# Clearing layer 0's semaphores inside three later stages, on GpSimd

## The chip, the core and the metric

The kernel runs on one core of a Trainium2 chip. The core has five engines, each with an instruction queue of its own: TensorE (matmuls, PE in the profile), VectorE (DVE), ScalarE (ACT), GpSimd (POOL) and SyncE (SP, which here only issues DMAs). They meet only through semaphores. The metric is the time of one execution on the device in microseconds, as the median of several runs.

## The reference

The trunk has two layers over 512 latent tokens and 256 context tokens of width 1024. Layer 0 mixes tokens by a gated convolution, layer 1 by a bidirectional gated recurrence (HGRN2). Each is followed by a retrieval of single-neuron experts (PEER). Cut to what matters:

```python
for i in range(DEPTH):                       # DEPTH = 2
    hx = modulate(rms_norm(x, norm1_g[i]), mx[0], mx[1])
    if kind == 0:
        yx = short_conv_mixer(hx, conv_w_in[j], conv_k[j], conv_w_out[j], rows)
    else:
        yc, yx = hgrn2_mixer(hc, hx, hgrn_w_in[j], lower_bounds[i], hgrn_norm_g[j], hgrn_w_out[j])
    x = x + mx[2] * yx
    x = x + mx[5] * peer_ffn(modulate(rms_norm(x, norm2_g[i]), mx[3], mx[4]),
                             peer_w_q[i], peer_keys[i], peer_u[i], peer_v[i])
    ...                                      # the context tokens in the same way in layer 0
return rms_norm(x, final_g)
```

`peer_ffn` projects each token to queries, ranks 128 + 128 keys for each of 8 heads, takes the 16 best pairs, and sums over those experts a gate times GELU(u . h) times v. The semaphores of the change compute nothing.

## The kernel before

The kernel is a row of stages, one after the other: `stage_front`, `stage_conv`, `stage_rank`, `stage_gates` and `stage_experts` for layer 0, then `stage_hgrn`, `stage_mix_out`, `stage_rank`, `stage_gates` and `stage_experts` for layer 1, then `stage_final`. Each stage is one `nc.Block()`: a list of instructions for each engine, which begin together and end with a barrier (each engine drains, then all are released together). The line of the `with nc.Block()` statement is the line under which the trace has these drains and releases: 1363 for `stage_experts`, 1610 for `stage_hgrn`, 108 for the block in `retire`.

Inside a stage the engines are ordered by semaphores which count up and are waited for with constants. A stage takes its semaphores with `t.sem(name)`, which also puts them on the list `t.own`. Weights flow in 512 KB tiles: SyncE loads a tile into one of four buffers (`w_raw`, line 131), ScalarE makes its high part (`w_hi`, line 136), VectorE or GpSimd the low part (`w_lo`, line 147, the helper `t.lo`), and TensorE multiplies three times (lines 168 to 170; 1426 to 1428 in the experts). The first two tiles of a stage are prepared at the end of the stage before.

The semaphores of layer 0's five stages are used again in layer 1, and must be zero for that. `retire()` (lines 106 to 115) is called once, between the layers: it opens a block of its own in which GpSimd clears each semaphore of `t.own` with one instruction (line 113), then empties the list and gives the semaphores back.

GpSimd's work in the three stages that the change touches is this. In `stage_gates` it waits for the expert indices of 128 tokens (`idx_done`) and then issues one gather for each expert row (line 1298), paced by VectorE. In `stage_experts` it zeroes the sums (line 1403), issues 256 gathers (line 1407) in layer 0, waits until the stage's weight tiles are done (`t.lo_done`), and makes the low parts of the next stage's first two tiles. In `stage_hgrn` it fills masks (lines 1619 to 1638) and then makes low parts of weight tiles, up to the first two of `stage_mix_out`; TensorE, ScalarE and VectorE run a loop of 3 passes over 2 heads each, and the last two heads after it. `stage_experts` has on TensorE, ScalarE, VectorE and SyncE a loop over groups of four tiles; VectorE's has 31 passes.

`stage_hgrn` begins with a norm: ScalarE takes a square root (line 434), VectorE a reciprocal (line 453), and then, slice by slice of 128 channels, VectorE scales (line 448), ScalarE makes the high part (line 438), VectorE the low part (line 462), and TensorE multiplies the slice.

Of the kernel before, what the change touches and what calls it, by code (L numbers as in the profile page):

```python
# [55 lines left out]
class Trunk:  # L56
# [46 lines left out]
        self.own.append(self.own_ctx.enter_context(self.nc.semaphore(name)))  # L103
        return self.own[-1]

    def retire(self):

        with self.nc.Block() as block:

            @block.gpsimd  # L110
            def _(pool):
                for s in self.own:
                    pool.sem_clear(s)
        self.own = []
        self.own_ctx.close()

    def settle(self, eng):

# [822 lines left out]
def stage_gates(t, layer, tokens, top, top_i, h_tok, idx, weight, g_dram, act_dram):  # L941
# [24 lines left out]
    with ExitStack() as ctx:  # L966
# [59 lines left out]
        with nc.Block() as block:  # L1026
# [178 lines left out]
            def _(act):  # L1205
# [54 lines left out]
                for i in range(SPLIT, W):  # L1260
                    t.hi(act, i, i, i, 0)
                h_copy(0)
                ends = [0] + [end for end, _, _ in order]
                wide_at = [{ends[n] + (ends[n + 1] - ends[n]) * x // 13: n for n in range(blocks)} for x in (2, 6)]
                exp_at = {ends[n] + (ends[n + 1] - ends[n]) * 8 // 13: n for n in range(blocks)}
# [23 lines left out]

            @block.gpsimd  # L1290
            def _(pool):
                rows = t.a[f"peer_u_rows{layer}"].rearrange("j i d -> (j i) d")
                for d in range(dots):
                    if d % P == 0:
                        pool.wait_ge(idx_done, d // P + 1)
                    if d >= UBUF:
                        pool.wait_ge(u_used, d - UBUF + 1)
                    pool.indirect_dma_start(  # L1298
                        out=ubuf[:, d % UBUF], out_offset=None, in_=rows,
                        in_offset=bass.IndirectOffsetOnAxis(ap=idx[:, d // P, d % P:d % P + 1], axis=0)).then_inc(  # L1300
                            u_in[d % UBUF], 16)
# [33 lines left out]
def stage_experts(t, layer, tokens, idx, weight, g_dram, act_dram, nxt=None):  # L1335
# [10 lines left out]
    with ExitStack() as ctx:  # L1346
# [16 lines left out]
        with nc.Block() as block:  # L1363
# [36 lines left out]
            @block.gpsimd  # L1400
            def _(pool):
                rows = t.a[f"peer_v{layer}"].rearrange("j i d -> (j i) d")
                pool.memset(acc[:], 0.0).then_inc(sum_zero, 1)
                for d in range(S * n):
                    if d >= NB:
                        pool.wait_ge(v_used, S + d - NB + 1)
                    pool.indirect_dma_start(  # L1407
                        out=vbuf[:, d % NB], out_offset=None, in_=rows,
                        in_offset=bass.IndirectOffsetOnAxis(ap=idx[:, d % S, d // S:d // S + 1], axis=0)).then_inc(
                            v_in[d % NB], 16)  # L1410
                if nxt is not None:
                    pool.wait_ge(t.lo_done, n + (t.tiles + RAW))
                    for x in range(SPLIT):
                        t.lo(pool, n + x, x, x)
# [135 lines left out]
def stage_hgrn(t, y, nxt, sums):  # L1550
# [21 lines left out]
    with ExitStack() as ctx:  # L1572
# [25 lines left out]
        def turns(eng, turn):  # L1598


            with eng.Fori(0, HEADS // 2 - 1) as q:
                for u in range(2):
                    turn(q, u, 1)
            turn(HEADS // 2 - 1, 0, 2)
            turn(HEADS // 2 - 1, 1, 0)
# [4 lines left out]
        with nc.Block() as block:  # L1610

            @block.sync
            def _(sp):
                for i in range(SPLIT, n + SPLIT):
                    t.load(sp, t.a["hgrn_w_in"][i] if i < n else nxt(i - n), i, i % N_RAW, N_RAW, None)

            @block.gpsimd
            def _(pool):
                pool.memset(reset[:], 1.0).then_inc(S["reset_done"], 1)
                for d in range(2):  # L1620
                    pool.memset(same[d][:], 1.0).then_inc(S["mask_done"], 1)
                    pool.memset(probs[d][:], 0.0).then_inc(S["reset_done"], 1)
                pool.wait_ge(S["reset_done"], 3)
                pool.memset(av(reset)[:, :, 0:1], 0.0).then_inc(S["reset_done"], 1)

                m = 2
                for d in range(2):
                    sv = same[d][:].rearrange("p (c l) -> p c l", l=CHUNK)
                    sign = 1 if d == 0 else -1

                    pool.wait_ge(S["mask_done"], m)
                    pool.affine_select(out=sv, in_=sv, compare_op=ALU.is_ge, fill=0.0, base=0,
                                       pattern=[[sign * CHUNK, P // CHUNK], [sign, CHUNK]],
                                       channel_multiplier=-sign).then_inc(S["mask_done"], 1)
                    m += 1

                    pool.wait_ge(S["mask_done"], m)
                    pool.affine_select(out=sv, in_=sv, compare_op=ALU.is_ge, fill=0.0,
                                       base=0 if d == 0 else CHUNK - 1,
                                       pattern=[[-sign * CHUNK, P // CHUNK], [0, CHUNK]],  # L1640
                                       channel_multiplier=sign).then_inc(S["mask_done"], 1)
                    m += 1

                def lo(q, j):
                    t.lo(pool, q * BODY + j, j % N_RAW, j % SPLIT)

                def turn(q, u, more):

                    if more:
                        for i in range(PER):  # L1650
                            lo(q, PER * (u + 1) + SPLIT + i)
                for j in range(SPLIT, PER + SPLIT):
                    lo(0, j)
                turns(pool, turn)

            @block.tensor
            def _(pe):
# [297 lines left out]
def hybrid_trunk(nc, a):  # L1955

    with ExitStack() as ctx:
        t = Trunk(nc, ctx, a)
        dense = [T - S * P for T, S in zip((TOK, SEQ), SPARSE)]
        g_dram = [nc.dram_tensor(f"gates{i}", [GROUPS, P, T // STAGE_T, QUAD * STAGE_T], F32, kind="Internal").ap()  # L1960
                  for i, T in enumerate(dense)]
        act_dram = [nc.dram_tensor(f"acts{i}", [NKEYS, P, T], F32, kind="Internal").ap() for i, T in enumerate(dense)]
        tile = lambda name: lambda x: a[name][x]
        for layer, tokens in enumerate((TOK, SEQ)):
            with ExitStack() as mix:
                t.context_h(mix, f"m{layer}")
                if layer == 0:
                    stage_front(t, tile("conv_w_in"))
                    y_hi = mix.enter_context(nc.sbuf_tensor("y_hi", [P, KC, TOK], F32R))
                    y_lo = mix.enter_context(nc.sbuf_tensor("y_lo", [P, KC, TOK], F32R))  # L1970
                    sums = stage_conv(t, y_hi, y_lo, tile("peer_w_q0"))
                else:
                    y = mix.enter_context(nc.sbuf_tensor("y_heads", [P, KC, SEQ], F32))
                    stage_hgrn(t, y, tile("hgrn_w_out"), sums)
                    sums = stage_mix_out(t, layer, "hgrn_w_out", tokens, t.moving(SEQ), tile("peer_w_q1"), SPLIT, y)
            with ExitStack() as pick:
                S = SPARSE[layer]
                sb = lambda n, s, d=F32: pick.enter_context(nc.sbuf_tensor(f"{n}{layer}", s, d))
                idx, weight = sb("expert_idx", [P, S, P], U32), sb("expert_weight", [P, S, P])
                with ExitStack() as lists:  # L1980
                    sb = lambda n, s, d=F32: lists.enter_context(nc.sbuf_tensor(f"{n}{layer}", s, d))
                    h_tok = sb("h_tok", [P, S, D])
                    top, top_i = sb("top", [P, tokens // P, LISTS, TOPK]), sb("top_i", [P, tokens // P, LISTS, TOPK], U32)
                    with ExitStack() as h:
                        if tokens == TOK:
                            t.context_h(h, f"p{layer}")
                        stage_rank(t, layer, tokens, top, top_i, h_tok, tile(f"peer_u{layer}"), sums)
                    stage_gates(t, layer, tokens, top, top_i, h_tok, idx, weight, g_dram[layer], act_dram[layer])
                sums = stage_experts(t, layer, tokens, idx, weight, g_dram[layer], act_dram[layer],
                                     tile("hgrn_w_in") if layer == 0 else None)  # L1990
            if layer == 0:
                t.retire()
        stage_final(t, sums)


# [58 lines left out]
```

## Time and profile before

| what | us |
|---|---|
| median of 3 runs | 4148.39 |
| lowest and highest run | 4147.36, 4149.64 |
| span of the profiled execution | 4139.5 |
| TensorE matmuls busy in it | 3881.7 |

The span goes from the first to the last instruction of the profiled execution; what a run takes beyond it lies before and after the program's instructions. Times in the rows are microseconds from the span's start unless marked ns. In a wait, "A <- B" says that A stood idle until B; an engine's name with a q (SPq, POOLq) is its instruction queue: waits, drains, clears and the issuing of DMAs, which aren't counted as busy.

### The profile page before, as it was taken

To read this page: it belongs to the slowest core of one execution; us is meant where nothing else is said; L and a number is where in the kernel's file an instruction comes from. 1 tells how busy PE (TensorE), PEld (TensorE's weight loads), DVE (VectorE), ACT (ScalarE), POOL (GpSimd) and SP (SyncE) were. 2 spreads that over 40 slices of the span, in tenths; PEclk is the share of its full clock that TensorE was granted. 3 is DMA by queue.
4 is the path that set the end of the run, shared out by engine and by line. 5 is a ranking of instruction groups with operands and counts; after the bars stand their busy time and mean duration, and the time that the engine had idled before them with its cause. 6 is when DMAs were issued, how large, how long until landed. Compare 5 with 4: busy or idle time off the path is not lost. (4 is left out here: it accounts for less than half of the span.)

```text
span 4139.5 us, 63328 instructions
## 1 busy us (share of the span) xinstructions
PE 3881.7 (94%) x20946; PEld 3333.0 (81%) x20946; DVE 3194.6 (77%) x5918; ACT 1963.3 (47%) x3786; POOL 1169.6 (28%) x905
## 2 busy tenths in 40 slices
PE   8998988999999989999997999778899999899998
PEld 2787877788888868888886777657899999899997
DVE  2698789999997768888886555658998877677777
ACT  2212234777777722222223555433488887333333
POOL 0232212343443334444442222123122222122221
PEclk9999999999999999999999999979999999999999
DMA  7443116899999999999991111022589898899996
GB/s 295 163 162 113 46 54 216 305 326 334 331 341 339 334 358 372 375 373 377 373 373 60 55 46 46 31 77 66 183 299 308 308 309 312 306 333 332 333 332 219
DMA packets 411884, 1026.09 MB, mean 248 GB/s; under 512 B 33968, under 2 KB 182448, under 8 KB 405680
## 3 DMA queue, kind: packets, MB, share of 16 engines
q1 hardware_dynamic: 296496, 604.22, 41.5%
q0 software_dynamic: 110592, 402.70, 26.8%
q10 hardware_dynamic: 4608, 16.78, 1.1%
q8 instruction: 104, 1.70, 0.2%
q14 instruction: 84, 0.69, 0.0%
HBM read 904.03 MB, written 119.54 MB: 247 GB/s over the span
## 5 line engine op out<-in xcount | busy, mean ns | idle before, releaser
L136 ACT ACTIVATE w_hi<-w_raw 128x1024 fp32r<-128x1024 f32 x536 | 568.3, 1060 | 1174.1 <-PE psum L1428 881.9
L168 PE MATMUL psum<-h_hi,w_hi 128*128 128x512 f32 (+1 forms) x2208 | 853.0, 386 | 89.6 <-PEq L809 32.8
L170 PE MATMUL psum<-h_hi,w_lo 128*128 128x512 f32 (+1 forms) x2208 | 832.5, 377 | 0.0
L169 PE MATMUL psum<-h_lo,w_hi 128*128 128x512 f32 (+1 forms) x2208 | 832.3, 377 | 0.0
L147 DVE TENSOR_TENSOR w_lo<-w_raw,w_hi 128x1024 fp32r<-128x1024 f32 x424 | 519.4, 1225 | 387.2 <-ACT w_hi L136 366.7
L1426 PE MATMUL psum<-a_hie,w_hi 128*128 128x512 f32 (+1 forms) x2048 | 756.6, 369 | 31.0 <-DVE a_loe L1499 31.0
L1428 PE MATMUL psum<-a_hie,w_lo 128*128 128x512 f32 (+1 forms) x2048 | 756.7, 369 | 0.0
L1427 PE MATMUL psum<-a_loe,w_hi 128*128 128x512 f32 (+1 forms) x2048 | 754.1, 368 | 0.0
L1298 POOL DMA_INDIRECT u_rowsg<-in_peer_u_rows,expert_idx x384 | 446.1, 1162 | 1050.9 <-DVE u_rowsg L1053 919.4
L1407 POOL DMA_INDIRECT v_rowse<-in_peer_v,expert_idx x384 | 421.1, 1097 | 830.1 <-DVE row_sume L1508 816.9
L1228 ACT ACTIVATE ojg<-eq_jg,gate_Tg 128x128 fp32r<-128x128 bf16 x1792 | 550.2, 388 | 109.9 <-DVE eq_jg L1076 109.4
L147 POOL TENSOR_TENSOR w_lo<-w_raw,w_hi 128x1024 fp32r<-128x1024 f32 x116 | 295.3, 2546 | 973.4 <-ACT w_hi L136 973.4
L168 PEld LDWEIGHTS psum<-h_hi,w_hi 128*128 128x128 f32 x2208 | 419.4, 190 | 142.5 <-issue 45.8
L1508 DVE SCALAR_TENSOR_TENSOR row_sume<-v_rowse,expert_weight,row_sume 128x1024 f32<-128x1024 f32 x384 | 491.0, 1279 | 0.3 <-DMA v_rowse<-in_peer_v,expert_idx 0.3
L1053 DVE SCALAR_TENSOR_TENSOR u_rowsg<-u_rowsg,psum 128x1024 f32<-128x1024 f32 x384 | 462.7, 1214 | 11.1 <-DMA u_rowsg<-in_peer_u_rows,expert_idx 7.6
L170 PEld LDWEIGHTS psum<-h_hi,w_lo 128*128 128x128 f32 x2208 | 418.6, 190 | 63.7
L1426 PEld LDWEIGHTS psum<-a_hie,w_hi 128*128 128x128 f32 x2048 | 385.5, 188 | 94.0 <-DVE a_loe L1499 32.2
L169 PEld LDWEIGHTS psum<-h_lo,w_hi 128*128 128x128 f32 x2208 | 420.0, 190 | 35.1
L1427 PEld LDWEIGHTS psum<-a_loe,w_hi 128*128 128x128 f32 x2048 | 385.8, 188 | 52.3
L1428 PEld LDWEIGHTS psum<-a_hie,w_lo 128*128 128x128 f32 x2048 | 385.5, 188 | 44.4
L1192 PEld LDWEIGHTS psum<-ojg,eq_ig 128*128 128x128 f32 x1792 | 230.8, 191 | 41.3 <-ACT ojg L1228 32.8
L168 PE MATMUL psum<-h_hi,w_hig 128*128 128x512 f32 (+1 forms) x672 | 253.5, 377 | 1.0 <-DVE w_log L147 0.9
(263 smaller groups left out, 5474.5 us busy)
## 6 DMA issues: line engine op xcount, KB each, us to landing
w_raw<-in_peer_u SPq DMA_DIRECT2D x256, 512.0 KB, 6.0
w_raw<-in_peer_v SPq DMA_DIRECT2D x256, 512.0 KB, 5.4
gates<-stageg SPq DMA_DIRECT2D x28, 2048.0 KB, 15.9
acts<-act_gg SPq DMA_DIRECT2D x128, 256.0 KB, 5.1
gte<-gates SPq DMA_DIRECT2D x32, 1024.0 KB, 8.3
act_fe<-acts SPq DMA_DIRECT2D x128, 256.0 KB, 6.0
ada_w<-in_ada_w SPq DMA_DIRECT2D x12, 2048.0 KB, 8.7
ada_rows<-in_ada_w SPq DMA_DIRECT2D x48, 512.0 KB, 3.8
```

The source lines that it names most:

```text
L136: act.activation(self.weights(s)[0], self.raw[:, slot, :], ACT.Copy).then_inc(self.hi_done, 1)
L147: pool.tensor_tensor(lo, self.raw[:, slot, :], hi.bitcast(F32), ALU.subtract).then_inc(self.lo_done, 1)
L168: pe.matmul(out, wh, hi[:, k], start=(k == 0), stop=False)
L169: pe.matmul(out, wh, lo[:, k], start=False, stop=False)
L170: last = pe.matmul(out, wl, hi[:, k], start=False, stop=(k == KC - 1))
L1053: dve.scalar_tensor_tensor(out=row, in0=row, scalar=1.0, in1=h_row, op0=ALU.mult, op1=ALU.mult, accum_out=pre_act[:, s, r:r + 1]).then_inc ...
L1228: last = act.activation(oj[:, g % OJ, x, j], eq_j[:, g % EQ, j], ACT.Copy, scale=gate_T[:, b % 2, x, r + j:r + j + 1])
L1298: pool.indirect_dma_start(out=ubuf[:, d % UBUF], out_offset=None, in_=rows, in_offset=bass.IndirectOffsetOnAxis(ap=idx[:, d // P, d % P:d ...
L1426: pe.matmul(out, vh, a_hi[:, s], start=(begin and i == 0), stop=False)
L1427: pe.matmul(out, vh, a_lo[:, s], start=False, stop=False)
L1428: last = pe.matmul(out, vl, a_hi[:, s], start=False, stop=(end and i == QUAD - 1))
L1508: dve.scalar_tensor_tensor(out=acc[:, s], in0=vbuf[:, slot], scalar=weight[:, s, bass.ds(c, 1)], in1=acc[:, s], op0=ALU.mult, op1=ALU.add) ...
```

## The change

`retire` is taken out. In its place `set_aside` moves the list of the semaphores used so far to `t.old`, `clear_old` has GpSimd clear what is on that list, and `free_old` gives them back. The semaphores of `stage_front` and `stage_conv` are set aside ahead of `stage_rank` and cleared as GpSimd's first instructions in layer 0's `stage_gates`; those of `stage_rank` and `stage_gates` are set aside behind `stage_gates` and cleared in layer 0's `stage_experts`, behind GpSimd's last gather and ahead of its wait for `t.lo_done`; those of `stage_experts` are set aside ahead of `stage_hgrn` and cleared as GpSimd's last instructions there.

```diff
-    def retire(self):
-
-        with self.nc.Block() as block:
-
-            @block.gpsimd
-            def _(pool):
-                for s in self.own:
-                    pool.sem_clear(s)
-        self.own = []
-        self.own_ctx.close()
+    def set_aside(self):
+
+        self.old, self.old_ctx = self.own, self.own_ctx
+        self.own, self.own_ctx = [], ExitStack()
+
+    def clear_old(self, pool):
+
+        for s in self.old:
+            pool.sem_clear(s)
+
+    def free_old(self):
+
+        self.old_ctx.close()
...
             @block.gpsimd
             def _(pool):
+                if layer == 0:
+                    t.clear_old(pool)
                 rows = t.a[f"peer_u_rows{layer}"].rearrange("j i d -> (j i) d")
                 for d in range(dots):
...
                 if nxt is not None:
+                    t.clear_old(pool)
                     pool.wait_ge(t.lo_done, n + (t.tiles + RAW))
                     for x in range(SPLIT):
                         t.lo(pool, n + x, x, x)
...
                 turns(pool, turn)
+                t.clear_old(pool)
...
+                    t.set_aside()
                     stage_hgrn(t, y, tile("hgrn_w_out"), sums)
+                    t.free_old()
...
+                        if layer == 0:
+                            t.set_aside()
                         stage_rank(t, layer, tokens, top, top_i, h_tok, tile(f"peer_u{layer}"), sums)
                     stage_gates(t, layer, tokens, top, top_i, h_tok, idx, weight, g_dram[layer], act_dram[layer])
+                    if layer == 0:
+                        t.free_old()
+                        t.set_aside()
                 sums = stage_experts(t, layer, tokens, idx, weight, g_dram[layer], act_dram[layer],
                                      tile("hgrn_w_in") if layer == 0 else None)
-            if layer == 0:
-                t.retire()
+                if layer == 0:
+                    t.free_old()
         stage_final(t, sums)
```

## Rows read from the trace of the kernel before

**Rows 1.** The page: span, and each engine's busy time, share, instructions.

```profile
span 4139.5 us, 63328 instructions
...
PE 3881.7 (94%) x20946; PEld 3333.0 (81%) x20946; DVE 3194.6 (77%) x5918; ACT 1963.3 (47%) x3786; POOL 1169.6 (28%) x905
```

**Rows 2.** Waits, 2195 to 2262: who waited for whom, total, times, longest.

```profile
ACT L434 <- PEq L108: 7.4, 1, 7.4
```

**Rows 3.** By line, line 113: count, ns min/median/max, first and last start.

```profile
L113 POOLq EVENT_SEMAPHORE_RANGE_CLEAR  x95: 37/38/47, 2215.3 to 2221.3; - x95
```

**Rows 4.** By line, line 108, the block of `retire`.

```profile
L108 POOLq DRAIN  x1: 53/53/53, 2221.4 to 2221.4; - x1
L108 SPq EVENT_SEMAPHORE  x1: 17/17/17, 2221.6 to 2221.6; - x1
```

**Rows 5.** Timeline, layer border: start, duration, engine, line, operation, [idle before].

```profile
2210.21 4.82 PE L1436 MATMUL psum<-sq_rowse,ones 128*128 128x256 f32 x16
...
2221.68 0.80 SPq L131 DMA_DIRECT2D w_raw<-in_hgrn_w_in  x2
```

**Rows 6.** By line, line 1363, the experts' blocks of layers 0 and 1.

```profile
L1363 SPq EVENT_SEMAPHORE  x2: 17/17/17, 2215.2 to 4126.0; - x2
```

**Rows 7.** Timeline, the borders ahead of `stage_mix_out` and of `stage_final`.

```profile
2712.27 0.94 DVE L1942 SCALAR_TENSOR_TENSOR y_heads<-psum,gains,zs 128x256 f32<-128x256 f32 x2 [0.33 <-PE psum L1730]
...
2713.70 1.75 SPq L131 DMA_DIRECT2D w_raw<-in_hgrn_w_out  x4
...
4125.09 0.71 PE L1436 MATMUL psum<-sq_rowse,ones 128*128 128x128 f32 x4 [0.23 <-ACT sq_rowse L1482]
...
4126.08 1.28 ACT L513 ACT_TABLE_LOAD   x1 [0.83 <-PEq L1363]
```

**Rows 8.** Timeline, `stage_gates` (first load, first gather), GpSimd in `stage_experts`, `stage_hgrn`.

```profile
596.42 0.33 SPq L131 DMA_DIRECT2D w_raw<-in_peer_u  x1
...
642.06 1.09 POOL L1298 DMA_INDIRECT u_rowsg<-in_peer_u_rows,expert_idx  x1 [58.92 <-DVEq L1161]
...
2176.82 1.14 POOL L1407 DMA_INDIRECT v_rowse<-in_peer_v,expert_idx  x1 [0.65 <-DVE row_sume L1508]
2194.92 3.14 POOL L147 TENSOR_TENSOR w_lo<-w_raw,w_hi 128x1024 fp32r<-128x1024 f32 x1 [16.95 <-ACT w_hi L136]
...
2668.15 2.60 POOL L147 TENSOR_TENSOR w_lo<-w_raw,w_hi 128x1024 fp32r<-128x1024 f32 x1 [11.68 <-ACT w_hi L136]
```

**Rows 9.** Timeline of VectorE and TensorE, the norm at the head of `stage_hgrn`.

```profile
2223.92 4.95 DVE L453 RECIPROCAL e<-e 128x768 f32<-128x768 f32 x1 [14.83 <-ACT e L434]
...
2246.08 0.48 DVE L462 SCALAR_TENSOR_TENSOR hc_lom<-b,mod,hc_him 128x256 fp32r<-128x256 f32 x1
...
2233.29 0.80 PE L168 MATMUL psum<-h_hi,w_hi 128*128 128x512 f32 x1 [18.25 <-DVE hc_lom L462]
...
2246.71 0.40 PE L168 MATMUL psum<-h_hi,w_hi 128*128 128x512 f32 x1
```

**Rows 10.** Stretches: length, busy us of each engine, PEclk (granted clock), DMA, GB/s.

```profile
2218.00:2219.00 1.00, 0.00 (x0) 0.00 (x0) 0.00 (x0) 0.00 (x0) 0.00 (x0) 1.00 0.00 0
2219.00:2220.00 1.00, 0.00 (x0) 0.00 (x0) 0.00 (x0) 0.00 (x0) 0.00 (x0) 0.53 0.00 0
2233.30:2239.30 6.00, 6.00 (x16) 4.64 (x17) 5.93 (x11) 2.64 (x6) 0.00 (x0) 0.50 0.00 0
```

**Rows 11.** Waits, 2660 to 2700, VectorE and TensorE, for nothing the trace shows.

```profile
DVE probs L1896 <- issue: 1.4, 1, 1.4
...
PE psum L1702 <- issue: 1.0, 1, 1.0
```

**Rows 12.** DMA queues (packets, MB, share): all of 2210-2224, 2400-2600; instructions in 3600-4100.

```profile
q1 hardware_dynamic: 63, 0.26, 9.5%
...
q1 hardware_dynamic: 2592, 9.44, 14.2%
...
q14 instruction: 1, 0.01, 0.0%
```

## The prediction

> **What bounds the kernel now.** I read the page first: TensorE's matmuls are busy for 94% of the 4139.5 us span [rows 1], so a change pays only where every engine, TensorE among them, stands still. Then I read the waits around the border between the layers. ScalarE idles 7.4 us before its first operation of `stage_hgrn`, with the line of the block that `retire` opens as its releaser [rows 2], and the reader is to see that no computing line is named: the stage waits for the block. Third, the block's own instructions by line: 95 clears on GpSimd from 2215.3 to 2221.3 us [rows 3], then GpSimd's drain at 2221.4 and the release of the others at 2221.6 [rows 4]. 95 is also what the code gives: 23 semaphores of `stage_front`, 21 of `stage_conv`, 16 of `stage_rank`, 21 of `stage_gates`, 14 of `stage_experts`. Fourth, the timeline at that border: TensorE's last product of `stage_experts` ends at 2210.21 + 4.82 = 2215.03 us and the first thing of `stage_hgrn`, a weight load on SyncE's queue, is issued at 2221.68 [rows 5]. The experts' own block released its engines at 2215.2 [rows 6]. So the whole chip stands for 6.65 us, and between the two releases lie 2221.6 - 2215.2 = 6.4 us which only the clears fill.
>
> **The block goes.** One clear after another comes every (2221.3 - 2215.3) / 94 = 0.064 us [rows 3], so 95 of them are 6.1 us, and drain and release add 0.3 [rows 4]: 6.4 us. The other side of that sum is what a border without such a block costs. From the layer-1 experts to `stage_final` it is 4126.08 - (4125.09 + 0.71) = 0.28 us from TensorE's end to ScalarE's start, and from `stage_hgrn` to `stage_mix_out` 2713.70 - (2712.27 + 0.94) = 0.49 us [rows 7]. 6.65 less these is 6.37 and 6.16. I take 6.4: the first border is the nearest, since the same stage ends in the same way there, and it agrees with the difference of the two releases.
>
> By a page's price the sum would be less. The Trainium skill, "Runtime: NRT & Kernel Launch", section "The ~15µs preamble/postamble breakdown", has an engine reset 51 semaphores in about 1.5 us; by that price, 0.029 us each (an estimate from that page), 95 clears and the 0.3 would be 3.1 us and the time 4145.3. The clears of this trace are twice as dear, and the measurement decides.
>
> **The clears come back in three places, at nothing.** All go on GpSimd's own queue, they wait for nothing, and no DMA moves with them. In `stage_gates` 44 of them (23 + 21) are 44 x 0.064 = 2.8 us at the head of the queue; GpSimd's next operation there is the first gather, which starts at 642.06 us after idling for the indices, while the stage's first weight load goes out at 596.42 [rows 8]. In `stage_experts` of layer 0, 37 (16 + 21) are 2.4 us behind the last gather, which is over at 2176.82 + 1.14 = 2177.96; behind them in the queue is the low part of two weight tiles (`w_lo`, line 147), which waits for ScalarE for 16.95 us, till 2194.92 [rows 8]. In `stage_hgrn` 14 are 0.9 us behind the last `w_lo`, which ends at 2668.15 + 2.60 = 2670.75 [rows 8], and the block closes only after VectorE's last operation at 2713.21 [rows 7]. So the covers are 45.6, 17 and 42 us for 2.8, 2.4 and 0.9. If a cover were gone, its clears would cost just these.
>
> **What is late next.** With the border shorter, SyncE's loads, GpSimd's memsets and ScalarE's square root of `stage_hgrn` all start 6.4 us earlier, and the chain behind is the same: VectorE's reciprocal (4.95 us) at 2223.92, then scaled rows in turn with high and low parts, and TensorE's first product at 2233.29 after 18.25 us of standing [rows 9]. VectorE's row by row pace sets that stretch: its last low part ends at 2246.08 + 0.48 = 2246.56 and TensorE starts the last slice at 2246.71 [rows 9]. Nothing in it refers to another clock than the release, so the whole of layer 1 moves forward as one piece. The granted TensorE clock is no second gain. It is still 1.00 at 2218 to 2219 us and 0.53 in the next, that is, it falls from 2.4 to 1.2 GHz some 4 us after the last product, and stays at 0.50 through 2233.3 to 2239.3 [rows 10]. After the change TensorE still stands for 18.25 - 6.4 = 11.9 us, beyond that fall, so the slow stretch stays; and were it gone, VectorE would set the same pace.
>
> **Unknown: the code moves.** A few instructions less on each engine shift all the code of layer 1. No row shows what that does; the nearest are two idle stretches in the last head of `stage_hgrn` which wait for nothing that the trace shows, 1.4 us on VectorE and 1.0 on TensorE [rows 11]. Such a stretch may vanish or come once more, so I price it at -2.4 to +2.4 us and take zero, as most of the stage has none.
>
> **Sum.** 4139.5 - 6.4 = 4133.1 us of span. Around the span lie 4148.39 - 4139.5 = 8.9 us, against the median of the runs; they stay. Time: 4142.0 us, 0.15% less.
>
> **Rivals.** First, the border was cover for something: reading the code of `stage_hgrn`. Then some or all of the 6.4 us comes back at its first instructions, and the time is between 4142.0 and 4148.4. For it speaks that those 6.4 us were free for such reads. Against it, in 2210 to 2224 us the only DMA queue with packets is the one of the weight loads [rows 12], and the two borders without the block start at once [rows 7].
>
> Second, the clears don't leave the path: in `stage_experts` they stand ahead of the two `w_lo`. For it, they are in the same queue. Against, 17 us of cover for 2.4. Time with that cover gone: 4142.0 + 2.4 = 4144.4.
>
> Third, slower: a loop of layer 1 whose code is now cut so that each pass has to read some of it again. The place is the 31 passes of the layer-1 experts' loop. At 1.4 us a pass [rows 11] that would be 43 us, less the 6.4 won: 4185. It decides from 6.4 / 31 = 0.21 us a pass on. In the three passes of the loop in `stage_hgrn` the same is 4.2 us and 4146.2. Against it, the loops of before read next to nothing: no instruction packet in 2400 to 2600 us, inside the loop of `stage_hgrn`, and one in 3600 to 4100 [rows 12], and few instructions are removed. The rule that speaks for it is in the Trainium skill, "Runtime: NRT & Kernel Launch", section "Instruction fetch mechanics": a taken branch whose target lies outside the pages that the engine holds must fetch it first. On the loops of before the trace shows no such fetch; whether the moved code has one, no row can tell.
>
> **How the numbers follow.** The forecast has a chance of 0.85, the first rival 0.06, the second 0.03, the slower one 0.06. The runs of before spread 2.3 us, so 1.2 to a side: the forecast's own range is 4142.0 - 2.4 - 1.2 = 4138.4 to 4145.6. I stretch the upper end to 4147.2, over the second rival, the three passes of `stage_hgrn` and most of the first rival. A measurement of this kernel can tell about 0.2% from no change, which is 8.3 us, from 4140.1 down or 4156.7 up. Faster than that needs 1.9 us on top of the forecast, the code's best case: 0.07, out of the forecast's 0.85. Slower is the third rival: 0.06. Within: 0.87.
>
> **What would show it.** In the changed kernel's trace `stage_hgrn` begins 0.3 to 0.5 us after the experts' last product, with no clears between; 44, 37 and 14 clears stand in the three stages, each run at about 0.064 us apart and over before GpSimd's next wait ends; the span is 6.4 us shorter and every later stage as long as before. A pause at the head of `stage_hgrn`, clears wider apart behind the gathers, a later `w_lo` at the end of `stage_experts`, or instruction packets inside a loop would prove me wrong.

## The result, and the profile after

The changed kernel takes 4158.05 us (median of 9 runs) where the kernel before takes 4148.39 (9 runs beside them): a ratio of 1.0021, 95% interval 1.0013 to 1.0030. It is slower, by 5 to 12 us, where 6.4 us less was forecast.

The page of the changed kernel (span; a queue of section 3 with packets, MB, share) and, for the same queue, that of the kernel before:

```profile
span 4145.9 us, 63317 instructions
...
q8 instruction: 122, 2.00, 0.2%
```

```profile
q8 instruction: 104, 1.70, 0.2%
```

q8 brings instructions, 16 KB a packet (2.00 MB / 122), and 18 packets more than before came. I had not made this line a part of the sum.

First the part that went as forecast. By line, the changed kernel's releases of `stage_experts` (line 1368, both layers) and `stage_hgrn` (line 1616), and its clears in the three stretches in which they now stand:

```profile
L1368 SPq EVENT_SEMAPHORE  x2: 17/17/17, 2214.0 to 4132.4; - x2
...
L1616 SPq EVENT_SEMAPHORE  x1: 17/17/17, 2722.7 to 2722.7; - x1
...
L114 POOLq EVENT_SEMAPHORE_RANGE_CLEAR  x44: 37/38/47, 597.2 to 600.0; - x44
...
L114 POOLq EVENT_SEMAPHORE_RANGE_CLEAR  x37: 37/38/43, 2175.3 to 2177.6; - x37
...
L114 POOLq EVENT_SEMAPHORE_RANGE_CLEAR  x14: 37/38/42, 2677.7 to 2678.5; - x14
```

The timeline of the changed kernel at the border, TensorE first (against [rows 5, 9]), and GpSimd's operations around the clears (against [rows 8]):

```profile
2208.93 4.82 PE L1442 MATMUL psum<-sq_rowse,ones 128*128 128x256 f32 x16
...
2214.02 0.80 SPq L134 DMA_DIRECT2D w_raw<-in_hgrn_w_in  x2
...
2214.04 1.28 ACT L437 ACT_TABLE_LOAD   x1 [1.04 <-PEq L1368]
...
2225.64 0.79 PE L171 MATMUL psum<-h_hi,w_hi 128*128 128x512 f32 x1 [11.88 <-DVE hc_lom L465]
...
643.50 1.09 POOL L1303 DMA_INDIRECT u_rowsg<-in_peer_u_rows,expert_idx  x1 [59.52 <-DVEq L1164]
...
2175.54 1.14 POOL L1412 DMA_INDIRECT v_rowse<-in_peer_v,expert_idx  x1 [0.66 <-DVE row_sume L1514]
2193.63 3.15 POOL L150 TENSOR_TENSOR w_lo<-w_raw,w_hi 128x1024 fp32r<-128x1024 f32 x1 [16.95 <-ACT w_hi L139]
...
2677.72 2.60 POOL L150 TENSOR_TENSOR w_lo<-w_raw,w_hi 128x1024 fp32r<-128x1024 f32 x1 [11.71 <-ACT w_hi L139]
```

The border is now 2214.02 - (2208.93 + 4.82) = 0.27 us, where it was 6.65, and TensorE idles 11.88 us instead of 18.25. The 44 clears are over 43 us before the first gather. The 37 do not even wait for the last gather: the first is issued at 2175.3, and the trace has that gather start at 2175.54. The `w_lo` behind them still waits 16.95 us for ScalarE, to the hundredth as before. The 14 are over at 2678.5, while the block closes at 2722.7.

Then the part that didn't. `stage_hgrn` took 2713.6 - 2221.6 = 492.0 us from release to release before and takes 2722.7 - 2214.0 = 508.7 now: 16.7 us more. The release that closed it before, by line:

```profile
L1610 SPq EVENT_SEMAPHORE  x1: 17/17/17, 2713.6 to 2713.6; - x1
```

TensorE's waits in that stage for which the trace shows no releaser (total, times, longest), after and before:

```profile
PE psum L171 <- issue: 12.8, 2, 6.5
```

```profile
PE psum L168 <- issue: 0.3, 2, 0.2
```

Where they are, by the timeline of TensorE, after and then before:

```profile
2378.72 0.97 PE L1737 MATMUL psum<-ident,e 128*128 128x128 f32 x4 [0.75 <-DVE e L1943]
2386.00 0.80 PE L171 MATMUL psum<-h_hi,w_hi 128*128 128x512 f32 x1 [6.32 <-issue]
...
2391.88 0.39 PE L171 MATMUL psum<-h_hi,w_hi 128*128 128x512 f32 x1
...
2506.84 0.79 PE L171 MATMUL psum<-h_hi,w_hi 128*128 128x512 f32 x1 [6.46 <-issue]
```

```profile
2387.40 0.49 PE L168 MATMUL psum<-h_hi,w_hi 128*128 128x512 f32 x1 [0.16 <-issue]
...
2390.66 0.39 PE L168 MATMUL psum<-h_hi,w_hi 128*128 128x512 f32 x1
...
2499.31 0.49 PE L168 MATMUL psum<-h_hi,w_hi 128*128 128x512 f32 x1 [0.16 <-issue]
```

Line 1737 (1730 before) is the last product of a pass of the loop, line 171 (168) the first of the next. Three passes have two returns to the loop's start, and both waits are at a return. A pass lasts 2506.84 - 2386.00 = 120.8 us instead of 2499.31 - 2387.40 = 111.9. The second return's wait, 6.46 for 0.16, is 6.3 of these 8.9 us; the rest is the clock behind the first return, by stretches of the changed kernel (the column behind POOL is the granted clock):

```profile
2378.00:2380.00 2.00, 0.87 (x4) 0.40 (x4) 1.66 (x6) 1.97 (x4) 0.00 (x0) 1.00 0.00 0
2382.00:2386.00 4.00, 0.00 (x1) 0.00 (x1) 4.00 (x3) 0.00 (x0) 2.13 (x1) 0.50 0.20 57
2386.00:2391.00 5.00, 5.00 (x15) 4.24 (x16) 0.15 (x1) 0.00 (x0) 0.00 (x0) 0.50 0.17 66
2391.60:2394.00 2.40, 2.40 (x15) 2.14 (x15) 0.00 (x0) 0.00 (x0) 0.00 (x0) 0.96 0.00 0
```

In the wait the clock falls from 2.4 to 1.2 GHz, and the next products run at it: from the first to the 19th it takes 2391.88 - 2386.00 = 5.88 us, where the kernel before takes 2390.66 - 2387.40 = 3.26, so 2.6 us are lost. And in the middle of the loop, 2400 to 2600 us, where no instruction packet came before [rows 12], the DMA view of the changed kernel now has:

```profile
q8 instruction: 14, 0.23, 0.5%
```

So TensorE's code of the loop is read again after a return. That q8 is TensorE's is shown below, where instructions on TensorE alone change its packets; the other instruction queue, q14, has 84 packets in every kernel of this case. That is my third rival, in the loop that I priced at 4.2 us and took into the range, at four times that price.

### The profile page after: what moved, and what is told of

Read it like the earlier page. It is cut to its first block and busy times, and to the rows that moved or that the text cites. A ratio compares the mean times of both kernels' runs of the same rounds, so it can differ in the third digit from the quotient of the medians.

```text
span 4145.9 us, 63317 instructions
## 1 busy us (share of the span) xinstructions
PE 3884.0 (94%) x20946; PEld 3335.4 (80%) x20946; DVE 3195.6 (77%) x5918; ACT 1963.2 (47%) x3786; POOL 1170.8 (28%) x905
## 5 line engine op out<-in xcount | busy, mean ns | idle before, releaser
L1514 DVE SCALAR_TENSOR_TENSOR row_sume<-v_rowse,expert_weight,row_sume 128x1024 f32<-128x1024 f32 x384 | 490.9, 1279 | 0.2 <-DMA v_rowse<-in_peer_v,expert_idx 0.2
## 6 DMA issues: line engine op xcount, KB each, us to landing
gates<-stageg SPq DMA_DIRECT2D x28, 2048.0 KB, 16.7
```

What stands on the lines that cost most here:

```text
L1514: dve.scalar_tensor_tensor(out=acc[:, s], in0=vbuf[:, slot], scalar=weight[:, s, bass.ds(c, 1)], in1=acc[:, s], op0=ALU.mult, op1=ALU.add) ...
```

## The experiments

Three theories of the 16.7 us. *The code's place*: `retire`'s block held two instructions on TensorE (drain and release); without them the loop of `stage_hgrn` lies two instructions earlier, and now doesn't fit into what TensorE holds of its code. *The clears*: in their new places they cost time. *The border*: 6.4 us of standing were needed to read code.

### An empty block put back

```diff
                 if layer == 0:
                     t.free_old()
+            if layer == 0:
+                with nc.Block():
+                    pass
```

> The changed kernel with an empty block put back between the layers: the clears stay where the change put them, and each engine gets back the block's drain and release, on TensorE two instructions. Theory (TensorE's code): the loss is in stage_hgrn's loop, whose code on TensorE has moved by those two instructions and must be read again in each pass; with them back, TensorE's waits for 'issue' at the two returns of the loop fall from 6.3 and 6.5 us to 0.2, queue q8 has the 104 packets of before instead of 122, stage_hgrn takes 492 us instead of 509, and the time is 4148.4 - 6.4 + 0.4 = 4142.4. Rival (the clears cost time inside the stages): as slow as the changed kernel, about 4158, with 122 packets or not. Rival (the border itself gave the time to read code): the block without clears is only some 0.4 us long, so still about 4158.

Measured: 4141.37 us, ratio to the time before 0.9986 (0.9977 to 0.9995); 104 packets on q8. TensorE's waits in `stage_hgrn`, and by line the end of the experts' block, the empty block's release and that of `stage_hgrn`:

```profile
PE psum L171 <- issue: 0.4, 2, 0.2
```

```profile
L1368 SPq EVENT_SEMAPHORE  x2: 17/17/17, 2221.5 to 4127.8; - x2
...
L2008 SPq EVENT_SEMAPHORE  x1: 17/17/17, 2221.9 to 2221.9; - x1
...
L1616 SPq EVENT_SEMAPHORE  x1: 17/17/17, 2715.5 to 2715.5; - x1
```

The block costs 0.4 us, the stage is back at 493.6, and the border is still 6 us shorter than before. So neither the clears in their new places nor the missing 6.4 us of the border cause the loss; but the block put instructions back on every engine.

### Two instructions put back on TensorE alone

```diff
+                for x in range(4):
+                    pe.wait_ge(t.tile_done, 1)
                 for k in range(KC):
                     norm.ready(pe, k)
                     tile(0, 0, 0, [k])
```

Two such waits go into one instruction, so four are two; here and below, numbers of instructions are those of the built program.

> The changed kernel with two instructions more on TensorE at the head of stage_hgrn, waits on a count that has long been reached; no block between the layers. Theory (TensorE's code): the loop of stage_hgrn lies again where it lay before, no waits for 'issue' of over 1 us at its returns, 104 packets on q8, 4142.0. Rivals (the clears in the stages, or the missing border): nothing changes, about 4158.

Measured: 4137.77 us, ratio 0.9981 (0.9971 to 0.9991), 104 packets, `stage_hgrn` 491.2 us, and these waits in it:

```profile
PE psum L171 <- issue: 0.4, 2, 0.3
```

Without any block: it is TensorE's code alone.

### The loss without the change

```diff
 # stage_front, TensorE
-                pe.sem_inc(t.lo_done, RAW)
-                pe.sem_inc(t.tile_done, SPLIT)
-                for x in range(2):
-                    pe.sem_inc(t.acc_free[x], 1)
 # stage_front, SyncE
+                sp.sem_inc(t.lo_done, RAW)
+                sp.sem_inc(t.tile_done, SPLIT)
+                for x in range(2):
+                    sp.sem_inc(t.acc_free[x], 1)
```

> The kernel before, with nothing of the change; only four semaphore increments at the head of stage_front go from TensorE to SyncE, so that TensorE's code from there on lies four instructions earlier. Theory (TensorE's code): the loop of stage_hgrn is read again in each pass, two waits for 'issue' of 6 us each, about 18 packets more on q8 than 104, stage_hgrn 509 us instead of 492: 4148.4 + 16.7 = 4165. Rivals (clears, border): no change from before, 4148.

Measured: 4160.92 us, ratio 1.0037 (1.0023 to 1.0050): 15 us more, where 16.7 were expected. The page's q8 line, the timeline at the two returns, and the releases around `stage_hgrn`:

```profile
q8 instruction: 122, 2.00, 0.2%
```

```profile
2400.50 0.79 PE L168 MATMUL psum<-h_hi,w_hi 128*128 128x512 f32 x1 [3.79 <-issue]
2403.28 0.79 PE L169 MATMUL psum<-h_lo,w_hi 128*128 128x512 f32 x1 [1.99 <-issue]
...
2520.61 0.79 PE L168 MATMUL psum<-h_hi,w_hi 128*128 128x512 f32 x1 [3.26 <-issue]
2523.56 0.79 PE L169 MATMUL psum<-h_lo,w_hi 128*128 128x512 f32 x1 [2.16 <-issue]
```

```profile
L108 SPq EVENT_SEMAPHORE  x1: 17/17/17, 2231.0 to 2231.0; - x1
...
L1610 SPq EVENT_SEMAPHORE  x1: 17/17/17, 2739.9 to 2739.9; - x1
```

508.9 us, and the same 122 packets, in a kernel whose clears stand where they stood. The wait now falls into two: one ahead of the loop's first product, one ahead of the second. In the program the loop's first four instructions are two that compute registers, a weight load and the first product. If these four lie at the end of one block of code and the next block is missing too, the second wait stands just where the trace has it.

### 245 instructions more

```diff
 # stage_front, TensorE, behind its four increments
+                for x in range(246):
+                    pe.wait_ge(t.tile_done, 1)
 # stage_hgrn, TensorE
+                for x in range(244):
+                    pe.wait_ge(t.tile_done, 1)
                 for k in range(KC):
```

> The changed kernel with 245 instructions more on TensorE ahead of the loop of stage_hgrn: 123 waits at the head of stage_front, where TensorE idles 10.5 us, and 122 at the head of stage_hgrn, where it idles 11.9; all on counts long reached. The theory (TensorE's code), if it is about where the loop's code lies against blocks of 16 KB (2.00 MB in 122 packets on q8): the loop crosses one block more at some starting points, and the place two instructions ahead of before's is among them. The Trainium skill, 'Runtime: NRT & Kernel Launch', section 'Instruction fetch mechanics', has 256 instructions in such a block; by that 245 more is 11 short of the same place, and the loop should be as badly placed as after the change, with waits for 'issue' of about 6 us at its returns and 4158 to 4165. If it is only a matter of having enough instructions ahead of the loop, the waits are gone and the time is 4142 plus what of the 245 is not hidden, at most some 5 us.

Measured: 4153.35 us, ratio 1.0015 (1.0005 to 1.0024), 123 packets, `stage_hgrn` 505.3 us. About as bad as forecast; of the 4.7 us by which the time lies under the 4158 given, 3.4 are in `stage_hgrn`, where the waits are shorter. The timeline at the returns:

```profile
2398.45 0.79 PE L171 MATMUL psum<-h_hi,w_hi 128*128 128x512 f32 x1 [3.40 <-issue]
2401.79 0.37 PE L173 MATMUL psum<-hc_him,w_lo 128*128 128x256 f32 x1 [1.28 <-issue]
...
2518.49 0.79 PE L171 MATMUL psum<-h_hi,w_hi 128*128 128x512 f32 x1 [3.67 <-issue]
2521.41 0.37 PE L173 MATMUL psum<-hc_him,w_lo 128*128 128x256 f32 x1 [0.85 <-issue]
```

The second wait has moved on to the sixth product. By the 256 instructions a block of the Trainium skill ("Runtime: NRT & Kernel Launch", "Instruction fetch mechanics"), 256 - 243 = 13 instructions of the loop were left to the block's end (an estimate): two that compute registers, five products with their weight loads, and the sixth's weight load. The trace agrees: the wait stands ahead of the sixth product.

### 120 more, one more

The same edit with 120 (60 and 60), and with one instruction in `stage_hgrn`.

> The control of the run with 245 more: the changed kernel with 120 instructions more on TensorE ahead of the loop of stage_hgrn, the same waits on counts long reached, 60 at the head of stage_front and 60 at the head of stage_hgrn. Theory (the loop's place against blocks of code): this place lies far from the bad one, so 104 or 105 packets on q8, no wait for 'issue' of over 1 us at the loop's returns, stage_hgrn some 492 us and 4142, less than 2 us off for waits that aren't hidden. If instead the 245 were slow because of their number: a loss of about half of the 13 us that stage_hgrn lost there, 4148.

Measured: 4146.43 us, ratio 0.9998 (0.9985 to 1.0011), 114 packets, `stage_hgrn` 497.5 us. Expected good, and it is half good: the first return costs nothing, the second does. Timeline:

```profile
2383.16 0.49 PE L171 MATMUL psum<-h_hi,w_hi 128*128 128x512 f32 x1 [0.23 <-issue]
...
2498.73 0.79 PE L171 MATMUL psum<-h_hi,w_hi 128*128 128x512 f32 x1 [3.88 <-issue]
```

This was my count. I had taken a pass of the loop as some 1300 instructions from the program. By stretches of the kernel before, one pass has 812 products and as many weight loads:

```profile
2387.30:2499.20 111.90, 102.51 (x812) 83.61 (x812) 63.96 (x145) 57.84 (x91) 25.96 (x10) 1.00 0.14 47
```

With some 60 others that is about 1690. The Trainium skill, "Runtime: NRT & Kernel Launch", section "Instruction fetch mechanics", gives a block of 16 KB 256 instructions. By that (an estimate) a pass is 6.6 blocks: begun at a block's first instruction it touches 7, begun in the last instructions of one, or more than about 100 behind its start, it touches 8. In these runs, seven are held and eight are not; 120 more, 118 beyond before's place, is just beyond. The count was fitted to the runs afterwards: that the good place ends near 100 is an estimate, and the runs show only that it ends between +58 and +118.

> The changed kernel with one instruction more on TensorE ahead of the loop of stage_hgrn, where two more brought it back. Theory: all or nothing. Either the loop's first instruction now opens a block: 104 packets on q8, no waits at the returns, 4142; or it is the last of one: 122 packets, one or two waits for 'issue' of 4 to 6.5 us at each of the two returns, about 4158. A theory in which each instruction has its share of the loss gives something between: 113 packets or waits of 3 us, 4150.

Measured: 4152.03 us, ratio 1.0013 (1.0001 to 1.0025), 122 packets, `stage_hgrn` 508.4 us, all of the loss. The timeline at the returns:

```profile
2393.12 0.79 PE L171 MATMUL psum<-h_hi,w_hi 128*128 128x512 f32 x1 [6.98 <-issue]
...
2514.11 0.79 PE L171 MATMUL psum<-h_hi,w_hi 128*128 128x512 f32 x1 [7.03 <-issue]
```

All or nothing: one instruction more is bad, two are good. So in the kernel before, by this count, the loop began exactly at the first instruction of a block, as the places of the second waits above say too.

### How wide the good place is

> The changed kernel with 60 instructions more on TensorE ahead of the loop of stage_hgrn (30 waits on counts long reached at the head of stage_front, 30 at the head of stage_hgrn), to see how wide the good place is: 2 more were good, 0 and 1 more bad, 120 more lost one of two returns. Theory (what is held of the code is a fixed number of blocks, and reading ahead at the loop's end drives its first block out): a block more is read ahead only once the loop's end lies deep enough in its last block; at 60 it lies less deep than at 120, so 104 packets and no wait at the returns over 1 us, stage_hgrn 492 us. If the good place is but a few instructions wide: 114 to 122 packets, waits of 4 to 6 us at one or both returns, stage_hgrn 497 to 509.

Measured, in a single run: 4136.51 us, 105 packets, waits of 0.3 us in sum, `stage_hgrn` 491.5.

> The same with 180 more (90 and 90). By the theory of reading ahead the loop's end lies deeper in its last block than at 120, so at least as bad: 114 to 122 packets, waits of 4 to 6 us at one or both returns, stage_hgrn 497 to 509 us. If 120 was a chance miss and places up to 234 are good: 104 packets, no waits, 492.

Measured, in a single run: 4152.84 us, 123 packets, `stage_hgrn` 504.2. Timeline:

```profile
2386.76 0.79 PE L171 MATMUL psum<-h_hi,w_hi 128*128 128x512 f32 x1 [3.85 <-issue]
...
2504.66 0.51 PE L171 MATMUL psum<-h_hi,w_hi 128*128 128x512 f32 x1 [3.62 <-issue]
```

Both as expected, though the corrected count explains them without the reading ahead that I had put into the expectation: 58 behind the start touches 7 blocks, 178 touches 8. All places together, from the start that the loop had in the kernel before:

| loop begins at | kernel | packets on q8 | `stage_hgrn`, us |
|---|---|---|---|
| -4 | before, four increments moved | 122 | 508.9 |
| -2 | the change | 122 | 508.7 |
| -1 | one more | 122 | 508.4 |
| 0 | before; empty block; two more | 104 | 492.0; 493.6; 491.2 |
| +58 | 60 more | 105 | 491.5 |
| +118 | 120 more | 114 | 497.5 |
| +178 | 180 more | 123 | 504.2 |
| +243 | 245 more | 123 | 505.3 |

At good places the stage repeats within 2.4 us; the loss is 5.5 to 17 us.

### The loop written out

```diff
 # stage_hgrn, TensorE
-                turns(pe, turn)
+                for q in range(HEADS // 2 - 1):
+                    for u in range(2):
+                        turn(q, u, 1)
+                turn(HEADS // 2 - 1, 0, 2)
+                turn(HEADS // 2 - 1, 1, 0)
```

> The changed kernel with TensorE's loop in stage_hgrn written out (three passes one behind the other, no return; the other engines keep their loops). Theory: what costs is the return to code that is no longer held, not the reading of code, which goes on ahead of a straight run. So q8 has more packets than 104, about 114 (two passes more of some 1300 instructions), no wait for 'issue' of over 1 us, stage_hgrn 492 us and 4142, whatever the place of the code. If the reading itself costs, through q8's packets, stage_hgrn stays near 505 and the time near 4155.

Measured: 4136.38 us, ratio 0.9976 (0.9965 to 0.9986): faster than both kernels. 117 packets, 13 more than 104, for two passes more of straight code: 2 x 1690 / 13 = 260 instructions a packet. By line, the releases around the stage (2710.6 - 2219.8 = 490.8 us):

```profile
L1368 SPq EVENT_SEMAPHORE  x2: 17/17/17, 2219.8 to 4123.9; - x2
...
L1616 SPq EVENT_SEMAPHORE  x1: 17/17/17, 2710.6 to 2710.6; - x1
```

In the stage no wait without a releaser is left over 1.0 us. The 13 packets of straight code cost nothing that can be seen in the stage (490.8 us beside 492.0); the return costs.

> The kernel before, block of clears and all, with TensorE's loop in stage_hgrn written out: beside the changed kernel with the same loop written out (0.9976 of the time before) it tells what the change itself is worth where the place of the code can't matter. Theory: the change is worth the 6.4 us of the border, so this one is at 0.9976 + 0.0015 = 0.9991 of the time before, with stage_hgrn at 491 us, about the 117 packets of the other and a border of 6.4 us. If the written-out loop was itself the gain: 0.9976 here too. If it was worth nothing: 1.0000.

Measured: 4144.38 us, ratio 0.9990 (0.9981 to 1.0000), `stage_hgrn` 490.9 us, 117 packets. Between the two kernels whose loop is written out lies the change alone, free of that loop's place: 0.9976 / 0.9990 = 0.9986, or 5.8 us, beside the 6.4 of the forecast and the same as the empty block gave. The two intervals taken together leave some 6 us to either side of it.

## Why the prediction was wrong

- *The block goes, 6.4 us*: right. The border is 0.27 us instead of 6.65. What the runs give for it, where the code's place is equal, is 0.9986 (empty block, written-out loops) and 0.9981 (two more): 6 to 8 us, and 6.4 lies within the interval of each.
- *The price of a reset by the Trainium skill ("Runtime: NRT & Kernel Launch", "The ~15µs preamble/postamble breakdown"), 0.029 us by estimate*: it didn't hold for these clears. They are as far apart in their new places as in the old one, where it was 0.064: (600.0 - 597.2) / 43 = 0.065.
- *The clears come back at nothing*: right in all three places; the waits that cover them are as long as before or longer, and `stage_hgrn` with the clears at its end and the code in place takes 491 us.
- *What is late next, the clock*: right. TensorE stands 11.88 us and starts at half clock as before.
- *Unknown: the code moves*: this is the step that failed. I saw that all of layer 1's code would move, named the loop of `stage_hgrn` as a place, and bounded the cost by idle stretches of 1.4 and 1.0 us that had nothing to do with it; I took zero. It was 16.7 us at two returns: 12.5 us more of waiting, and most of the rest half clock behind the waits. So layer 1 did not move forward as one piece, and one of the prediction's own signs of being wrong, instruction packets inside a loop, is what the trace has.
- *The third rival*: the mechanism was the right one, its chance (0.06, and that in the experts' loop) and its price were wrong. Against it I had put that the loop of before reads no code in 2400 to 2600 us [rows 12]. That row tells that the loop was held; it tells nothing of how near it was to not being held. Rows that would have warned were there: 812 products and weight loads in a pass, and q8 reading 16 KB at a time, make a loop of nearly 7 blocks, long enough for its place to matter. That 7 blocks are held and 8 are not, so that only about 100 of 256 places leave the loop whole (an estimate), no row of the kernel before tells; it took the runs above. And "few instructions are removed" counts for nothing where one is enough.
- *The first and second rival*: neither came. The first is ruled out by TensorE's 11.88 us at the head of the stage, shorter by all of the border, and by the empty block and the two instructions; the second by the 16.95 us wait.
- *The sum and the range*: The 8.9 us around the span were not that. The changed kernel's execution of 4145.9 us of span took 4147.72, 1.8 more; so the profiled execution of before was one of some 4141, under its median. It did no harm, as it stood on both sides. The spread of the runs did: 2.3 us in three, but 4140.5 to 4153.2 in nine. The measured 4158.05 lies outside the range of 4138.4 to 4147.2 because of the code's place: without the 16.7 us it would be 4141.4, beside the 4142.0 forecast.

## What to carry to other kernels

Before a change takes or adds instructions ahead of a long loop, count what an engine runs in one pass (products and weight loads from the stretches view) against what it holds, and see on the instruction queues of the DMA view whether the loop is read again; a change on another engine altogether can move it. If the loop is near the limit, write it out or make it shorter rather than pad it: the padded kernel is fast until the next edit. And measure such a change with the place of the code held equal (an empty block, two idle instructions), or a gain of 6 us is read as a loss of 10.

## What the runs showed of the hardware

- TensorE kept a loop of about 1690 instructions over its returns when it lay on 7 blocks of 16 KB by the estimate above, and read it again when it lay on 8: 9 packets a return (18 more on q8 for two). Why 9 and not 8 is not shown. By the same section of the Trainium skill TensorE holds 128 KB, 8 such blocks, which would let the loop fit anywhere; the runs at -4, -2, -1, +178 and +243 speak against that. What takes the eighth is not shown, nor why +118 lost only its second return.
- A return to code that was gone cost 3.6 to 7.0 us of waiting: a first wait of 3.3 to 3.9 us, with a second of 0.9 to 2.2 us where by the count the next block began within a few products, or one wait of 6.3 to 7.0 us where it began ahead of the first product. Behind the changed kernel's first return the half clock lost another 2.6 us.
- A block with nothing in it costs 0.4 us between two stages.
- The runs of one kernel differ by more than 10 us. Each kernel has one trace, so where its own runs differ can't be read. Between kernels, layer 0's `stage_gates` differs by as much: from release to release it took 1470.6 - 597.2 = 873.4 us in the changed kernel's profiled execution and 884.0 in that of the kernel before with four increments moved, which has no clears there. By line, that kernel's releases:

```profile
L809 SPq EVENT_SEMAPHORE  x2: 17/17/17, 597.4 to 2929.0; - x2
...
L1026 SPq EVENT_SEMAPHORE  x2: 17/17/17, 1481.4 to 3582.4; - x2
```

The kernel before has the spread of its runs without the change; what causes it is open.
